# One encoder layer on one core: the last down group in token halves, and the early modulation mixed of split and unsplit chunks

## The chip, the core and the metric

The kernel runs on one core of one Trainium2 chip. The metric is the device time of one execution in microseconds; three runs of the kernel before gave 2707.13 to 2711.16 us, median 2709.91 us. All times below are microseconds from the start of the span unless marked otherwise. PE is TensorE, ACT ScalarE, DVE VectorE, POOL GpSimd and SP SyncE; here SP only issues transfers.

## The reference, cut to what matters

One layer (DEPTH = 1) over 512 prompt tokens and 32 sample tokens of width D_MODEL = 2048, in float32:

```python
mod = cs @ w_mod[li] + b_mod[li]                      # cs = silu(c), 2 rows; w_mod 2048 x 12288
sh_a, sc_a, gt_a, sh_f, sc_f, gt_f = [...]            # six pieces of 2048
h = rmsnorm(x, g_attn[li]) * (1.0 + sc_a) + sh_a
z = h @ w_in[li]
...
x = x + gt_a * o
h2 = rmsnorm(x, g_ffn[li]) * (1.0 + sc_f) + sh_f
f, cnew = conv_ffn(h2, cstate, w_up[li], conv_w[li], conv_b[li], w_down[li])
x = x + gt_f * f
y = rmsnorm(x, g_final)                               # the final norm
```

The attention between z and o and the convolution in conv_ffn are not touched. w_down is 5632 x 2048.

## The kernel before

All tokens, 544 of them, are kept transposed: 16 tiles (kt) of 128 features by 544 tokens. The large products are done as three float32r matmuls of split operands, hi x hi, hi x lo and lo x hi. For a weight chunk of 128 x 1024, ACT copies `w_raw` to `w_hi` (`hi`), and DVE subtracts that from `w_raw` to make `w_lo` (`lo`). There are four `w_raw` slots, four `w_hi` and four `w_lo`. Each engine runs its own hand-written program in order; semaphores join them.

**The early stage.** Of `w_mod` the first 32 of 96 column tiles (shift and scale of the attention norm) are done before the projection, as 64 chunks e = 0 to 63 of 512 KB, 8 to a group. PE multiplies a chunk unsplit, as float32, with `cs` (128 x 2) as the stationary operand and the chunk's two 512-column halves as moving ones. Each of these two matmuls is two records in the trace, so a chunk is four. After each group ACT copies the 2 x 512 result out (`group_out`), and PE turns it into columns (`group_columns`, L1542, after chunk 8g+1), to which DVE adds the bias (`group_mod`). While chunks 8 to 23 pass, PE also transposes x: after chunk e the tile kt = e - 8 (L1575 and L1576); ACT squares and copies it (L835, L836), DVE sums the squares. After chunk 28 PE sums them over the features (L1533), ACT takes the root (L801), DVE the reciprocal (L1205). Then DVE makes hT (`h_mul`, L1168), ACT x_hi (`h_hi`, L817) and DVE x_lo (`h_lo`, L1177) for each tile; the last four tiles wait for the last group's columns. The projection (L1584 to L1586) starts after chunk 63.

SP issues all loads in one list, `STREAM`. The load that fills a slot waits for the chunk four places earlier in the list to be used: for a modulation chunk that is `m_used`, which PE raises. Chunk e sits in slot e % 4 up to e = 61.

**The last stage.** The feed-forward part runs in 11 groups of 4 hidden tiles. The last group's down product (`down`) makes 16 output tiles n, each in two token halves (272 + 272) in turn, from 8 weight chunks. DVE adds each half into x1 (`gated`) and multiplies a finished tile by g_final (xg, L1504); ACT squares it (L1056), POOL sums the squares over the tiles (L766), PE transposes xg back to token rows (`y_turn`, L1806), and ACT copies them to `y_nat` (L1062, L1064). When all tiles are done, PE sums the squares over features for all tokens (L1821), ACT takes the root (L1083), DVE the reciprocal, and five row tiles of `y_nat` are scaled, two on ACT (L1089) and three on DVE (L1515), and stored by SP (L579, L581). The convolution's last positions (`u_rows`) are stored by POOL at the very end.

Of the kernel before, what the change touches and what calls it, by code (L numbers as in the profile page):

```python
# [223 lines left out]
W_AT = 62  # L224

# [76 lines left out]
SC0 = FC0  # L302
assert len(STREAM) % NR == FC0 % NR == EC % NR == HEAD % NR == 0
LOOP_CHUNKS = 2 * GRP * 6
LAST_DOWN = 4 * GRP + LOOP_CHUNKS * (NG - 1) // 2
ROW_COUNTS = [2 * KT, MOD_TILES, 3 * KT] + [2 * FT] * 6


def build(nc, A, O):
# [5 lines left out]
    with ctx:  # L315
# [40 lines left out]
        mod_rows = [on(st0, f"mod_rows{i}", [2, EG]) for i in range(2)]  # L356
# [37 lines left out]
        fin_st = ExitStack()  # L394
        xg = [on(fin_st, f"xg{i}", [P, T]) for i in range(2)]
        fin_st.close()
# [24 lines left out]
        f_sq, f_sum = cv, ext[1][:, 0:T]  # L421
# [24 lines left out]
        scratch_out = [sem(f"scratch_out{i}") for i in range(2)]  # L446
        ld_c, e_ev, e_t, e_tev = sem("ld_c"), sem("e_ev"), sem("e_t"), sem("e_tev")
# [45 lines left out]
        def _(sp):  # L493
            def slot_free(old):

                if old[0] == "w":
                    sp.wait_ge(s_lo, old[1] + 1)
                elif old[0] == "e":
                    sp.wait_ge(m_used, old[1] + 1)
                else:  # L500
                    sp.wait_ge(late_d, LK * (old[1] + 1))
                    sp.wait_ge(late_act, old[1] + 1)
# [74 lines left out]
            for t, ready, n in ((0, f_scd, 1), (2, f_sca, 1), (1, f_scd, 2), (3, f_sca, 2)):  # L577
                sp.wait_ge(ready, n)
                sp.dma_start(O["y_p"][0, P * t:P * t + P, :], y_nat[:, t, :]).then_inc(store, 16)  # L579
# [6 lines left out]
        def _(pool):  # L586
# [13 lines left out]
            pool.memset(minus_half, -0.5).then_inc(consts, 1)  # L600
            tiled = lambda a: a.rearrange("(k p) -> k p", p=P)
# [175 lines left out]
        def _(act):  # L777
# [18 lines left out]
            act.wait_ge(consts, 4)  # L796
# [11 lines left out]
            def hi_early(c):  # L808
                if c >= NW:
                    act.wait_ge(g_done, 2 * ((c - NW) // 2) + 2)  # L810
                hi(c, RAW_OF[("w", c)] % NR, LOADED[("w", c)])
# [9 lines left out]
            def group_out(g):  # L821

                act.wait_ge(m_used, EPG * (g + 1))
                if g >= 2:
                    act.wait_ge(e_t, g - 1)
                act.activation(mod_rows[g % 2][:, :], bank(7 - g % 2)[0:2, :], ACT.Copy).then_inc(e_ev, 1)

            for kt in range(KT):
                if (X_AT + kt) % EPG == 0:
                    group_out((X_AT + kt) // EPG - 1)  # L830
# [6 lines left out]
                if kt == 0:  # L837
# [7 lines left out]
            for kt in range(EGT, 2 * EGT):  # L845
                h_hi(kt)
            group_out(4)
            group_out(5)
            for kt in range(2 * EGT, 3 * EGT):
                h_hi(kt)  # L850
            group_out(6)
            hi_early(0)
            hi_early(1)
            group_out(7)
# [196 lines left out]
            def squares(kts):  # L1051
                for kt in kts:
                    act.wait_ge(d_ev, 4 + 8 * GRP * (NG - 1) + 2 * kt + 2)
                    if kt >= 2:
                        act.wait_ge(f_add, kt - 1)
                    act.activation(f_sq[kt % 2][:, 0:T], x1[:, kt, :], ACT.Square).then_inc(f_square, 1)  # L1056

            def y_out(kts):
                for kt in kts:
                    act.wait_ge(f_t, kt + 1)  # L1060
                    b = 2 * (kt % 2)
                    act.activation(y_nat[:, 0:QT, P * kt:P * kt + P],  # L1062
                                   bank(b)[:, :].rearrange("p (t n) -> p t n", n=P), ACT.Copy)
                    act.activation(y_nat[0:TS, QT, P * kt:P * kt + P], bank(b + 1)[0:TS, 0:P], ACT.Copy  # L1064
                                   ).then_inc(f_ev, 1)


            base = 8 * GRP * (NG - 1)
            act.wait_ge(d_done, base - 4)
            hi_ffn((LAST_DOWN + 2, None))  # L1070
            act.wait_ge(d_done, base)
            hi_ffn((LAST_DOWN + 3, None))
            for n in range(8):
                if n + 4 < 8:
                    act.wait_ge(d_done, base + 4 * (n + 1))
                    hi_ffn((LAST_DOWN + n + 4, None))
                squares(range(2 * n, 2 * n + 2))
                if n:
                    y_out(range(2 * n - 2, 2 * n))
            y_out(range(KT - 2, KT))  # L1080

            act.wait_ge(f_sum_t, 1)
            act.activation(tiny[:, 8:8 + QT], bank(0)[:, 0:QT], ACT.Sqrt, bias=eps, scale=1.0 / D)  # L1083
            act.activation(tiny[0:TS, 8 + QT:9 + QT], bank(0)[0:TS, QT:QT + 1], ACT.Sqrt, bias=eps[0:TS, :],
                           scale=1.0 / D).then_inc(f_sd, 1)
            act.wait_ge(f_rs, 1)
            act.wait_ge(f_ev, KT)
            for t in (2, 3):
                act.activation(y_nat[:, t, :], y_nat[:, t, :], ACT.Copy, scale=tiny[:, 8 + t:9 + t]).then_inc(f_sca, 1)  # L1089

            act.wait_ge(uc_t, 1)
            act.activation(u_rows[0:2 * FT, :, :].rearrange("p r n -> p (r n)"), bank(3)[0:2 * FT, :], ACT.Copy
                           ).then_inc(uc_ev, 1)
# [3 lines left out]
        def _(dve):  # L1097
# [83 lines left out]

            dve.wait_ge(rows_t, len(ROW_COUNTS))
            for i in range(1, len(ROW_COUNTS)):
                row_out(i)
            dve.wait_ge(ld_small, 80)
            for i in range(2):
                a, b = lam[2 * i], lam[2 * i + 1]
                dve.tensor_tensor_reduce(a[:, :], a[:, :], b[:, :], 1.0, 0.0, ALU.mult, ALU.add,
                                         tiny[:, 6 + i:7 + i]).then_inc(lam_dot, 1)
            dve.wait_ge(rows_ev, len(ROW_COUNTS))  # L1190
            group_mod(0)
            for kt in range(1, KT):
# [6 lines left out]
            dve.wait_ge(lam_exp, 1)  # L1199
            step(dve.tensor_tensor(tiny[:, 3:4], tiny[:, 5:6], tiny[:, 4:5], ALU.subtract))  # L1200
            step(dve.tensor_scalar(neg_lam, tiny[:, 3:4], -LAMBDA_INIT, None, ALU.add))
            group_mod(1)
            group_mod(2)
            dve.wait_ge(sd_ok, 1)
            dve.reciprocal(n0_rstd[:, :], n0_rstd[:, :]).then_inc(rs_ok, 1)  # L1205
            dve.wait_ge(rs_ok, 1)
            for q in range(4):
                for g in range(max(3, 2 * q), 2 * q + 2):
                    if g == E_GROUPS - 1:
                        lo(0, RAW_OF[("w", 0)] % NR, 0)  # L1210
                        lo(1, RAW_OF[("w", 1)] % NR, 1)
                    group_mod(g)
                dve.wait_ge(mod_ok, q + 1)
                for kt in range(EGT * q, EGT * q + EGT):
                    h_mul(kt)
                    if kt >= 2:
                        h_lo(kt - 2)
            h_lo(KT - 2)
            h_lo(KT - 1)

            def lo_early(c):
                lo(c, RAW_OF[("w", c)] % NR, c)
# [271 lines left out]

            lo_ffn((LAST_DOWN + 2, None))
            lo_ffn((LAST_DOWN + 3, None))
            for n in range(8):
                for q in range(4 * (n % 2), 4 * (n % 2) + 4):
                    down_out(q, n // 2, GRP * (NG - 1) + n // 2)
                for kt in (2 * n, 2 * n + 1):  # L1500
                    dve.wait_ge(d_ev, 4 + 8 * GRP * (NG - 1) + 2 * kt + 2)
                    if kt >= 2:
                        dve.wait_ge(f_t, kt - 1)
                    dve.tensor_scalar(xg[kt % 2][:, :], x1[:, kt, :], cols[:, GT, 2 * KT + kt:2 * KT + kt + 1], None,  # L1504
                                      ALU.mult).then_inc(f_mul, 1)
                if n + 4 < 8:
                    lo_ffn((LAST_DOWN + n + 4, None))
            dve.wait_ge(f_sd, 1)
            dve.reciprocal(tiny[:, 8:8 + QT], tiny[:, 8:8 + QT])
# [346 lines left out]
```

## Time and profile before

| what | value |
|---|---|
| median of the three runs | 2709.91 us |
| the profiled execution's own time | 2706.82 us |
| its span | 2705.0 us |
| PE busy, share of the span | 2619.0 us, 97% |
| DVE, ACT, POOL busy | 60%, 35%, 19% |
| first projection product on PE | 156.2 us |
| last product of the last down group starts | 2681.5 us |
| scaling of the output rows starts | 2688.0 us |

The profiled execution spends 1.82 us outside its span. A share of busy time is a mean over stages of different limits: this change is in the first 165 and the last 80 of 2705 us, and only what ends last there counts.

### The profile page before, as it was taken

To read this page: it belongs to the slowest core of one execution; us is meant where nothing else is said; L and a number is where in the kernel's file an instruction comes from. 1 tells how busy PE (TensorE), PEld (TensorE's weight loads), DVE (VectorE), ACT (ScalarE), POOL (GpSimd) and SP (SyncE) were. 2 spreads that over 40 slices of the span, in tenths; PEclk is the share of its full clock that TensorE was granted. 3 is DMA by queue.
4 is the path that set the end of the run, shared out by engine and by line. 5 is a ranking of instruction groups with operands and counts; after the bars stand their busy time and mean duration, and the time that the engine had idled before them with its cause. 6 is when DMAs were issued, how large, how long until landed. Compare 5 with 4: busy or idle time off the path is not lost.

```text
span 2705.0 us, 50278 instructions
## 1 busy us (share of the span) xinstructions
PE 2619.0 (97%) x19783; PEld 2448.8 (91%) x19783; DVE 1634.6 (60%) x3210; ACT 958.4 (35%) x1871; POOL 524.9 (19%) x461
## 2 busy tenths in 40 slices
PE   7999999999999999999999999999999999999997
PEld 2268889898988999899999999999999999999997
DVE  1469889874357888965554555555455555445554
ACT  2236666664344335422222222222222222222224
POOL 1057777761003452400000000000000000000003
PEclk9999999999999999999999999999999999999998
DMA  8886556562215654432332332233232223223231
GB/s 256 265 266 192 172 181 182 171 161 60 59 48 160 172 164 125 148 110 81 92 94 84 90 93 80 80 94 94 79 94 83 82 88 94 87 86 94 79 94 70
DMA packets 416210, 324.96 MB, mean 120 GB/s; under 512 B 44410, under 2 KB 360218, under 8 KB 414880
## 3 DMA queue, kind: packets, MB, share of 16 engines
q1 hardware_dynamic: 410032, 302.55, 37.6%
q0 software_dynamic: 5248, 14.56, 1.7%
q10 hardware_dynamic: 688, 4.47, 0.5%
q8 instruction: 169, 2.77, 0.4%
q14 instruction: 73, 0.60, 0.1%
HBM read 307.67 MB, written 14.07 MB: 119 GB/s over the span
## 4 chain that ended last, share of the span: by engine, by line
PE 84%; DVE 7%; DMA 3%; issue 2%; POOL 2%; ACT 1%; SPq 1%; ACTq 0%; DVEq 0%; POOLq 0%
PE ps L1584 25%; PE ps L1586 24%; PE ps L1585 24%; PE ps L1558 4%; DVE late_f L1256 3%; PE ps L1673 2%; PE ps L1639 2%; DMA w_raw<-in_w_out 2%; DMA w_raw<-in_w_mod 1%; PE ps L1657 1%; POOL oT L708 1%; DVE w_lo L1149 1%; SPq L547 1%; ACT w_hi L806 1%; PE ps L1595 1%
## 5 line engine op out<-in xcount | busy, mean ns | idle before, releaser
L1584 PE MATMUL ps<-x_hi,w_hi 128*128 128x272 f32 (+1 forms) x4480 | 1320.1, 295 | 32.1 <-DVE w_lo L1149 22.5
L1585 PE MATMUL ps<-x_lo,w_hi 128*128 128x272 f32 (+1 forms) x4480 | 1298.2, 290 | 0.0
L1586 PE MATMUL ps<-x_hi,w_lo 128*128 128x272 f32 (+1 forms) x4480 | 1296.2, 289 | 0.0
L1584 PEld LDWEIGHTS ps<-x_hi,w_hi 128*128 128x128 f32 x4480 | 850.3, 190 | 45.9 <-issue 27.6
L1586 PEld LDWEIGHTS ps<-x_hi,w_lo 128*128 128x128 f32 x4480 | 852.0, 190 | 0.0
L1585 PEld LDWEIGHTS ps<-x_lo,w_hi 128*128 128x128 f32 x4480 | 849.8, 190 | 0.0
L806 ACT ACTIVATE w_hi<-w_raw 128x1024 fp32r<-128x1024 f32 x368 | 375.0, 1052 | 1049.6 <-PE ps L1586 901.5
L1149 DVE TENSOR_TENSOR w_lo<-w_raw,w_hi 128x1024 fp32r<-128x1024 f32 x368 | 456.6, 1270 | 343.1 <-ACT w_hi L806 342.7
L1586 PE MATMUL ps<-y_hi,w_lo 128*128 128x272 f32 x1408 | 406.8, 289 | 0.0
L1584 PE MATMUL ps<-y_hi,w_hi 128*128 128x272 f32 x1408 | 406.1, 288 | 0.0
L1585 PE MATMUL ps<-y_lo,w_hi 128*128 128x272 f32 x1408 | 404.5, 287 | 0.0
L763 POOL TENSOR_TENSOR ext<-cv 128x544 f32<-128x544 f32 x1 | 1.5, 1509 | 1479.4 <-ACT cv L1056 1479.4
L1585 PEld LDWEIGHTS ps<-y_lo,w_hi 128*128 128x128 f32 x1408 | 265.3, 188 | 0.0
L1586 PEld LDWEIGHTS ps<-y_hi,w_lo 128*128 128x128 f32 x1408 | 264.7, 188 | 0.0
L1584 PEld LDWEIGHTS ps<-y_hi,w_hi 128*128 128x128 f32 x1408 | 264.6, 188 | 0.1
L1358 DVE SCALAR_TENSOR_TENSOR x<-ps,mod,x 128x272 f32<-128x272 f32 (+2 forms) x576 | 204.1, 399 | 69.8 <-PE ps L1586 69.8
L708 POOL TENSOR_TENSOR oT<-oT 128x512 f32<-128x512 f32 x150 | 223.7, 1492 | 33.7 <-ACT oT L870 25.7
L1415 DVE COPY u_shift<-ps 128x2 f32<-128x2 f32 x88 | 13.9, 158 | 307.4 <-PE ps L1586 307.4
L1256 DVE SCALAR_TENSOR_TENSOR oT<-w_raw,cs,oT 128x512 f32<-128x512 f32 x150 | 178.6, 1191 | 2.8
L708 POOL TENSOR_TENSOR late_f<-late_f 128x512 f32<-128x512 f32 x90 | 136.7, 1519 | 180.5 <-ACT late_f L870 175.8
L1558 PE MATMUL ps<-w_raw,cs 128*2 128x512 f32 x256 | 119.5, 614 | 13.8 <-DMA w_raw<-in_w_mod 13.1
L1256 DVE SCALAR_TENSOR_TENSOR late_f<-w_raw,cs,late_f 128x512 f32<-128x512 f32 x90 | 122.1, 1356 | 3.6 <-DMA w_raw<-in_w_mod 0.5
(195 smaller groups left out, 2095.8 us busy)
## 6 DMA issues: line engine op xcount, KB each, us to landing
w_raw<-in_w_mod SPq DMA_DIRECT2D x192, 512.0 KB, 4.6
w_raw<-in_w_up SPq DMA_DIRECT2D x176, 512.0 KB, 4.6
w_raw<-in_w_down SPq DMA_DIRECT2D x88, 512.0 KB, 4.2
w_raw<-in_w_in SPq DMA_DIRECT2D x56, 512.0 KB, 3.9
w_raw<-in_w_in SPq DMA_DIRECT2D x32, 256.0 KB, 3.7
w_raw<-in_w_out SPq DMA_DIRECT2D x16, 512.0 KB, 5.3
w_raw<-in_w_out SPq DMA_DIRECT2D x64, 128.0 KB, 3.9
x_transposed<-xT SPq DMA_DIRECT2D x4, 1088.0 KB, 8.6
```

The lines of the kernel that those rows point to most:

```text
L547: sp.dma_start(dst[64 * u:64 * u + 64, 4 * m:4 * m + 4, :], src.rearrange("(i p) n -> p i n", p=64)).then_inc(ld_raw[slot], 16)
L708: ins = pool.tensor_tensor(acc, late_prod(n, 0) if p == 0 and k == 1 else acc, late_prod(n, k), ALU.add)
L806: act.activation(w_hi[c % NW][:, :], w_raw[raw][:, :], ACT.Copy).then_inc(s_hi, 1)
L1149: dve.tensor_tensor(w_lo[c % NW][:, :], w_raw[raw][:, :], w_hi[c % NW][:, :].bitcast(F32), ALU.subtract).then_inc(s_lo, 1)
L1256: ins = dve.scalar_tensor_tensor(out=acc_d(g), in0=w, scalar=c, in1=acc_d(g), op0=ALU.mult, op1=ALU.add)
L1358: ins = dve.scalar_tensor_tensor(out=x1[:, n, a:a + m], in0=b[:, a - HALF[h][0]:a - HALF[h][0] + m], scalar=mod[:, gate + n, g:g + 1], in1 ...
L1558: mm = pe.matmul(bank(7 - g % 2)[0:2, :], cs[:, kt, :], w_raw[raw][:, EG * k:EG * k + EG], start=kt == 0, stop=kt == KT - 1)
L1584: pe.matmul(out[:, 0:n], hi_w, hi_x, start=first, stop=False)
L1585: pe.matmul(out[:, 0:n], hi_w, lo_x, start=False, stop=False)
L1586: return pe.matmul(out[:, 0:n], lo_w, hi_x, start=False, stop=last)
L1639: mm = pe.matmul(S[t % 2][0:np_, pc:pc + n], zq[qi % 2][r, q0:q0 + np_], kk, start=True, stop=True)
L1673: mm = pe.matmul(B7[0:np_, oc:oc + vn], probsT[0:n, tc:tc + np_], v, start=first, stop=last)
```

## The change

It has two parts.

**Early modulation.** The odd chunks from 7 to 59 (27 of 64) are split into hi and lo like the other weights, in the same `w_hi`/`w_lo` buffers, and PE multiplies them with float32r matmuls, four a chunk, against `c_parts`, 128 x 4, which holds the hi and lo parts of cs. The other chunks are still multiplied as float32, against `c_whole` (cs and two columns of zeros). The result has four rows, which `group_columns` adds by a matmul with `pair` (two stacked 2 x 2 identities) in place of a transpose. ACT and DVE get the conversions three chunks ahead (`AHEAD`), and the h work of tiles 0 to 11 is tied to places in the chunk sequence (`H_AT`). A slot of a split chunk is free when its lo part is made (`s_lo`), and not when PE has used it.

**Last down group.** All 16 tiles are done for the first 272 tokens, then all for the second (`down_last(h, n)`). The first 256 tokens' squares, root, scaling and store run beside the second half. The eight weight chunks stay on the core for both passes, the later ones in y_hi, y_lo and x_lo (`tail_w`).

```diff
+SPLIT = range(7, 60, 2)
+AHEAD = 3
+H_AT = {SUM_AT + 3: 0, SUM_AT + 4: 2, 36: 4, 37: 6, 52: 8, 53: 10}
...
                 if old[0] == "w":
-                    sp.wait_ge(s_lo, old[1] + 1)
+                    sp.wait_ge(s_lo, ES + old[1] + 1)
+                elif old[0] == "e" and old[1] in SPLIT:
+                    sp.wait_ge(s_lo, SPLIT.index(old[1]) + 1)
                 elif old[0] == "e":
                     sp.wait_ge(m_used, old[1] + 1)
...
-            group_out(2)
-            root(0, n0_rstd[:, :])
-            for kt in range(EGT):
-                h_hi(kt)
-            group_out(3)
...
+            def hi_split(e):
+
+                n = SPLIT.index(e)
+                if n >= NW:
+                    act.wait_ge(m_used, SPLIT[n - NW] + 1)
+                hi(n, RAW_OF[("e", e)] % NR, LOADED[("e", e)])
...
+            for e in range(EC):
+                if e + AHEAD in SPLIT:
+                    hi_split(e + AHEAD)
+                if e % EPG == 1 and e > EPG:
+                    group_out(e // EPG - 1)
+                if 0 <= e - X_AT < KT:
+                    x_in(e - X_AT)
...
+                if e == SUM_AT + 1:
+                    root(0, n0_rstd[:, :])
+                if e in H_AT:
+                    h_hi(H_AT[e])
+                    h_hi(H_AT[e] + 1)
...
+            for e in range(EC):
+                if e + AHEAD in SPLIT:
+                    lo_split(e + AHEAD)
...
+                if e == SUM_AT + 2:
...
+                    dve.reciprocal(n0_rstd[:, :], n0_rstd[:, :]).then_inc(rs_ok, 1)
+                    dve.wait_ge(rs_ok, 1)
+                if e in H_AT:
+                    dve.wait_ge(mod_ok, H_AT[e] // EGT + 1)
+                    h_mul(H_AT[e])
+                    h_mul(H_AT[e] + 1)
+                if e - 1 in H_AT:
+                    h_lo(H_AT[e - 1])
+                    h_lo(H_AT[e - 1] + 1)
...
+                    if e in SPLIT:
+                        n = SPLIT.index(e) % NW
+                        pe.matmul(bank(7 - g % 2)[0:4, :], c_parts[:, kt, :], w_hi[n][:, EG * k:EG * k + EG],
+                                  start=kt == 0, stop=False)
+                        mm = pe.matmul(bank(7 - g % 2)[0:4, :], c_parts[:, kt, :], w_lo[n][:, EG * k:EG * k + EG],
+                                       start=False, stop=kt == KT - 1)
+                    else:
+                        mm = pe.matmul(bank(7 - g % 2)[0:4, :], c_whole[:, kt, :], w_raw[raw][:, EG * k:EG * k + EG],
+                                       start=kt == 0, stop=kt == KT - 1)
...
+            for h in range(2):
+                for n in range(KT):
+                    down_last(h, n)
+                    if n % 2 and n > 1:
+                        y_turn(h, n - 3)
+                        y_turn(h, n - 2)
+                    if h and n == 1:
+                        y_turn(0, KT - 2)
+                        y_turn(0, KT - 1)
+                    if h and n == 3:
+                        token_sums(0)
...
+            y_turn(1, KT - 2)
+            y_turn(1, KT - 1)
+            token_sums(1)
```

What ACT has in its order from the root of the first norm on, before (in a row's brackets stand the semaphores that it waits for):

```order
L801 ACTIVATE n_rstd<-ps,tiny 128x544 [waits ss_ok]
L817 ACTIVATE x_hi<-hT,mod 128x512 [waits n_mul]
L817 ACTIVATE x_hi<-hT,mod 128x32
L817 ACTIVATE x_hi<-hT,mod 128x512 [waits n_mul]
L817 ACTIVATE x_hi<-hT,mod 128x32
L817 ACTIVATE x_hi<-hT,mod 128x512 [waits n_mul]
L817 ACTIVATE x_hi<-hT,mod 128x32
L817 ACTIVATE x_hi<-hT,mod 128x512 [waits n_mul]
L817 ACTIVATE x_hi<-hT,mod 128x32
L826 ACTIVATE mod_rows<-ps 2x512 [waits e_t,m_used]
```

The same place on ACT now; the three rows of L841 are `hi_split` of chunks 33, 35 and 37, L854 is `h_hi`, L863 `group_out(3)`:

```order
L836 ACTIVATE n_rstd<-ps,tiny 128x544 [waits ss_ok]
L841 ACTIVATE w_hi<-w_raw 128x1024 [waits ld_raw1,m_used]
L854 ACTIVATE x_hi<-hT,mod 128x512 [waits n_mul]
L854 ACTIVATE x_hi<-hT,mod 128x32
L854 ACTIVATE x_hi<-hT,mod 128x512 [waits n_mul]
L854 ACTIVATE x_hi<-hT,mod 128x32
L841 ACTIVATE w_hi<-w_raw 128x1024 [waits ld_raw3,m_used]
L854 ACTIVATE x_hi<-hT,mod 128x512 [waits n_mul]
L854 ACTIVATE x_hi<-hT,mod 128x32
L854 ACTIVATE x_hi<-hT,mod 128x512 [waits n_mul]
L854 ACTIVATE x_hi<-hT,mod 128x32
L863 ACTIVATE mod_rows<-ps 4x512 [waits e_t,m_used]
```

Conversions of weight chunks now stand between the x_hi rows, and the copy-out of group 3 stands behind a conversion and four tiles of x_hi, as before behind four tiles.

DVE from there on now (L1220 is `lo_split`: chunks 31, 33 and later 35; L1239 is `h_mul`):

```order
L1220 TENSOR_TENSOR w_lo<-w_raw,w_hi 128x1024 [waits s_hi] x2
L1289 TENSOR_TENSOR tiny<-tiny 128x1 [waits lam_exp]
L1290 TENSOR_SCALAR tiny<-tiny 128x1 [waits dve_own]
L1292 RECIPROCAL n_rstd<-n_rstd 128x544 [waits sd_ok,dve_own]
L1239 SCALAR_TENSOR_TENSOR hT<-xT,mod,n_rstd 128x512 [waits mod_ok,rs_ok]
L1239 SCALAR_TENSOR_TENSOR hT<-xT,mod,n_rstd 128x32
L1239 SCALAR_TENSOR_TENSOR hT<-xT,mod,n_rstd 128x512
L1239 SCALAR_TENSOR_TENSOR hT<-xT,mod,n_rstd 128x32
L1220 TENSOR_TENSOR w_lo<-w_raw,w_hi 128x1024 [waits s_hi]
L1239 SCALAR_TENSOR_TENSOR hT<-xT,mod,n_rstd 128x512 [waits mod_ok]
```

Before, the reciprocal stood right behind the sums of squares and two groups' columns, and nothing of the weights stood between it and hT.

The order of SP's loads from chunk 32 on now:

```order
L542 DMA w_raw<-in_w_mod 128x2x512 [waits m_used]
L542 DMA w_raw<-in_w_mod 128x2x512 [waits s_lo]
L542 DMA w_raw<-in_w_mod 128x2x512 [waits m_used]
L542 DMA w_raw<-in_w_mod 128x2x512 [waits s_lo]
```

Before, every one of them waited for `m_used` of the chunk four places earlier. Now an odd chunk's load waits for a lo part, and for the even chunk's load ahead of it in the list.

## Rows read from the trace of the kernel before

**Rows 1.** The page: busy time, share of the span, instructions, by engine.

```profile
PE 2619.0 (97%) x19783; PEld 2448.8 (91%) x19783; DVE 1634.6 (60%) x3210; ACT 958.4 (35%) x1871; POOL 524.9 (19%) x461
```

**Rows 2.** Windows: stretch and its length, busy us (instructions), granted clock, DMA share, GB/s.

```profile
36.60:76.60 40.00, 40.00 (x150) 13.30 (x150) 10.39 (x16) 19.03 (x33) 0.00 (x0) 1.00 0.70 210
97.40:140.00 42.60, 42.60 (x109) 8.76 (x108) 14.54 (x42) 9.25 (x19) 0.00 (x0) 1.00 0.86 285
```

**Rows 3.** Chain of work, start, length, what: one chunk with transposes of x.

```profile
42.93 1.81 PE ps L1558 x4
44.74 0.59 PE ps L1575 x4
45.33 0.17 PE ps L1576
```

**Rows 4.** Chain of work: one group of 8 chunks without them.

```profile
125.78 13.96 PE ps L1558 x32
```

**Rows 5.** SP's loads of w_mod, by issue in 42 to 74 us, then 99 to 148 us.

```profile
DMA to landing us min/median/max: 4.2/4.4/4.8
...
DMA to landing us min/median/max: 3.7/4.7/5.0
```

**Rows 6.** Conversions of one chunk, hi on ACT and lo on DVE, ns min/median/max.

```profile
L806 ACT ACTIVATE w_hi<-w_raw x10: 1038/1059/1064, 2602.8 to 2653.3; 128x1024 fp32r<-128x1024 f32 x10
...
L1149 DVE TENSOR_TENSOR w_lo<-w_raw,w_hi x11: 1214/1218/1225, 2599.1 to 2654.9; 128x1024 fp32r<-128x1024 f32 x11
```

**Rows 7.** Window in which PE does nothing but split products of 272 and 274 columns.

```profile
2580.00:2600.00 20.00, 20.00 (x161) 20.00 (x161) 12.22 (x24) 4.78 (x8) 0.00 (x0) 1.00 0.17 53
```

**Rows 8.** Groups by line, 0 to 190 us: x coming in on ACT.

```profile
L835 ACT ACTIVATE n_sq<-ps 128x544 f32<-128x544 f32 x16 | 10.0, 624 | 22.0 <-PE ps L1576 22.0
L836 ACT ACTIVATE xT<-ps 128x544 f32<-128x544 f32 x16 | 9.9, 618 | 0.0
```

**Rows 9.** Chain of work after chunk 28: sums, root, reciprocal, hT, columns of group 3.

```profile
85.77 1.06 PE ps L1533 x2
...
87.00 0.72 ACT n_rstd L801
...
87.75 3.56 DVE n_rstd L1205
...
91.33 2.57 DVE hT L1168 x6
...
97.05 0.40 PE ps L1542 x4
```

**Rows 10.** Chain of work around the last two chunks.

```profile
145.35 4.61 DMA w_raw<-in_w_mod
...
155.19 0.60 ACT mod_rows L826
```

**Rows 11.** Windows of the same place, with the granted clock.

```profile
143.00:149.70 6.70, 4.03 (x10) 0.68 (x8) 1.46 (x2) 2.11 (x2) 0.00 (x0) 1.00 0.95 300
149.70:153.10 3.40, 3.10 (x4) 0.47 (x5) 0.99 (x1) 0.00 (x0) 0.00 (x0) 0.51 0.77 240
```

**Rows 12.** Chain of work: the first of ACT's two scalings of 2048 elements.

```profile
2688.04 2.00 ACT y_nat L1089
```

**Rows 13.** Timeline of PE behind the last transposes.

```profile
2686.10 1.21 PE L1821 MATMUL ps<-ones,ext 128*128 128x1 f32 x10 [0.84 <-ACT y_nat L1064]
2687.23 0.68 PE L1825 MATMUL ps<-ident,u_last 128*88 128x128 f32 x4
```

**Rows 14.** Windows in the last down group, and of the stores.

```profile
2650.00:2660.00 10.00, 10.00 (x84) 9.98 (x82) 5.42 (x12) 5.82 (x13) 5.32 (x4) 1.00 0.01 2
...
2692.00:2700.00 8.00, 0.00 (x0) 0.00 (x0) 0.00 (x0) 0.42 (x1) 2.11 (x4) 0.50 1.01 392
2700.00:2703.00 3.00, 0.00 (x0) 0.00 (x0) 0.00 (x0) 0.00 (x0) 0.00 (x0) 0.50 0.83 238
2703.00:2705.00 2.00, 0.00 (x0) 0.00 (x0) 0.00 (x0) 0.00 (x0) 0.00 (x0) 0.50 0.00 0
```

More of the change, by code:

```diff
@@ L355, in build @@
         lam = [on(st0, f"lambda{i}", [P, A_DK]) for i in range(4)]
-        mod_rows = [on(st0, f"mod_rows{i}", [2, EG]) for i in range(2)]
+        mod_rows = [on(st0, f"mod_rows{i}", [4, EG]) for i in range(2)]
+        c_parts = on(st0, "c_parts", [P, KT, 4], F32R)
+        c_whole = on(st0, "c_whole", [P, KT, 4])
+        pair = on(st0, "pair", [P, 2])
         st0.close()
@@ L825, in group_out, with x_in @@
                     act.wait_ge(e_t, g - 1)
[L826 to L830, printed above, removed]
+                act.activation(mod_rows[g % 2][:, :], bank(7 - g % 2)[0:4, :], ACT.Copy).then_inc(e_ev, 1)
+            def hi_split(e):
[3 more added lines that the diff above has]
+                hi(n, RAW_OF[("e", e)] % NR, LOADED[("e", e)])
+            def x_in(kt):
                 act.wait_ge(xt_t, kt + 1)
@@ new lines, in _ @@
+            act.wait_ge(d_done, DOWN0 - 4)
+            hi_last(2)
+            act.wait_ge(d_done, DOWN0)
+            hi_last(3)
+            act.wait_ge(u_done, 4 * FT)
+            for h in range(2):
+                for n in range(8):
+                    if h == 0 and n + 4 < 8:
+                        hi_last(n + 4)
+                    for kt in (2 * n, 2 * n + 1):
+                        squares(h, kt)
+                    if n:
+                        y_out(h, 2 * n - 2)
+                        y_out(h, 2 * n - 1)
+                    elif h:
+                        y_out(0, KT - 2)
+                        y_out(0, KT - 1)
+                    if h and n == 2:
+                        final_root(0)
+                    if h and n == 4:
+                        final_scale(0)
+                    if h and n == 5:
+                        act.wait_ge(uc_t, 1)
+                        act.activation(u_rows[0:2 * FT, :, :].rearrange("p r n -> p (r n)"), bank(3)[0:2 * FT, :],
+                                       ACT.Copy).then_inc(uc_ev, 1)
@@ L1180, in h_lo, with lo_split, sum_row @@
                 ins.then_inc(x_ok, 1)
[L1182 to L1192, printed above, removed]
+            def lo_split(e):
+                n = SPLIT.index(e)
+                lo(n, RAW_OF[("e", e)] % NR, n)
+            def sum_row(kt):
                 dve.wait_ge(sq_mul, kt + 1)
@@ L1198, in _ @@
                 ins.then_inc(sq_ok if kt == KT - 1 else sq_add, 1)
[L1199 to L1217, printed above, removed]
@@ L1221, in lo_early @@
+            lo(0, RAW_OF[("w", 0)] % NR, ES)
+            lo(1, RAW_OF[("w", 1)] % NR, ES + 1)
+            group_mod(E_GROUPS - 1)
+            dve.wait_ge(mod_ok, KT // EGT)
+            for kt in range(3 * EGT, KT):
+                h_mul(kt)
+            for kt in range(3 * EGT, KT):
+                h_lo(kt)
             def lo_early(c):
-                lo(c, RAW_OF[("w", c)] % NR, c)
+                lo(c, RAW_OF[("w", c)] % NR, ES + c)
             def late_cols(tile, n, b):
@@ L1541, in group_columns @@
                 for t in range(EGT):
[L1542 to L1543 removed]
+                    mm = pe.matmul(bank(5)[:, 2 * t:2 * t + 2], mod_rows[g % 2][0:4, P * t:P * t + P], pair[0:4, :],
+                                   start=True, stop=True)
                 mm.then_inc(e_t, 1)
```

294 lines of the change are left out of this document (177 added, 117 removed).

## Prediction

> **What bounds the kernel now.** I read the page first: PE is busy 97% of the span [rows 1], so at almost any place time is gained only by taking work from PE, and lost by anything that makes PE wait. Then the windows of the early stage: with x coming in and without it PE has no idle time at full clock, at a DMA share of 0.70 and 0.86 [rows 2]. The chain of waits shows the same in single pieces: with transposes a chunk is 1.81 + 0.59 + 0.17 = 2.57 us of PE [rows 3]; without them eight are 13.96 us, 1.74 each [rows 4], 14.2 with the columns. The change takes PE work from here. So the question is what else can deliver chunks, and how fast: SP's loads [rows 5] and the conversions on ACT and DVE [rows 6].
>
> **What a split chunk saves.** In a window of nothing but split products PE starts 161 in 20.0 us [rows 7], 0.124 us for 272 columns; by columns 0.234 us for 512, so four are 0.94 us in place of 1.74. 27 chunks give 21 us back if PE never waits. The columns of a group (0.40 us) cost the same as a matmul.
>
> **How fast split chunks can come.** Let e be even. Slots e and e+1 are refilled by the loads e+4 and e+5, which stand in this order on SP; the first waits for PE to end chunk e, so the second can't go earlier either, although its slot has been free since its lo part was made. A load lands 4.4 us after its issue where the queue is light, 4.7 where it is loaded [rows 5]. At a share of 0.86 the queue moves 285 GB/s [rows 2], so full it moves 331, and the second of two loads is 524 KB / 331 GB/s = 1.6 us behind: 6.1 us after PE's end of e with the issue. Then 1.06 us hi, 1.22 us lo [rows 6] and 0.1 us of semaphores: PE can begin chunk e+5 no sooner than 8.5 us after the end of chunk e, and from there to there are four chunks. That is 4.25 us for a pair of chunks. Before, an even and an odd chunk took 5.14 us with transposes and 3.5 us without. The rule thus gives something only while x comes in (PE's own work is there 1.74 + 0.94 + 2 x 0.76 = 4.2 us a pair), and costs something in the rest. Before, the same load had three chunks of PE's time to come in, 5.2 us, with no conversion behind it.
>
> The Trainium skill (DMA: Bandwidth & Descriptors, Anatomy of one DMA) puts a DMA at about 2.0 us and bytes over 436 GB/s, 3.2 us for such a chunk. The trace has 4.4 [rows 5] and decides. By the page the rule above would give 0.1 + 3.2 + 1.2 + 2.4 = 6.9 us for two pairs, and a stretch without transposes would not grow.
>
> **The sum, by stretches of chunks, from PE's side.**
> Chunks 8 to 28: eight pairs with transposes, 8 x (4.25 - 5.14) = -7.1 us. But ACT has `group_out` behind `hi_split` of chunk 8g+3 and, at 9 and 17, behind one tile of x (0.62 + 0.62 us [rows 8]). Counted from the end of chunk 8g-2, ACT is through after 6.1 + 1.1 + 1.2 + 0.6 + 0.1 = 9.1 us, and PE, which has the columns right behind chunk 8g+1, stands there after 5.9. Three such waits (3.2, 3.2, and 2.8 without the tile of x) are +9.2. Sum +2.1.
> Chunks 29 to 33: the place in the order of ACT and DVE shown above. From the end of chunk 28: load 33 is in after 6.6 (the queue still has 31), hi and lo 33 make it 9.0; only then does DVE come to the reciprocal, 3.56 and two tiny operations: 12.9; h_mul 0 and 1 (2.57 for three, 0.86 each) 14.6; h_hi 1 15.5; hi 35 16.5; lo 35 17.8; h_mul 2 and 3 19.5; h_hi 3 20.4; `group_out` 3 21.0; columns 21.4. Before it was 97.05 + 0.40 - 85.77 = 11.7 us [rows 9], since root and reciprocal began at 87.00 and 87.75 with no conversion ahead. +9.7.
> Chunks 34 to 41: chunk 34 is 1.74, the rule brings lo 39 at 10.2; then four h_mul 3.4, h_hi 7 0.9, hi 41 1.1 (it stands behind them on ACT), lo 41 1.2: 16.9; chunk 41 and columns 18.3, against 14.2: +4.1. Chunks 50 to 57 have the same order: +4.1.
> Chunks 42 to 49: two times 8.5 is 17.0, against 14.2: +2.8.
> Chunk 58 to the last tile of the first projection product: one split chunk fewer than it costs now (-0.8); the wait for load 62 and the group's copy-out stay [rows 10], since 60 to 63 are unsplit; DVE's last four tiles no longer have h_lo 10 and 11 between them (-1.1): -1.9.
> At full clock: 2.1 + 9.7 + 4.1 + 4.1 + 2.8 - 1.9 = +20.9 us. Nothing after this stage starts by the clock on the wall: the projection, its tables and its loads all wait for x_lo, so it is passed on whole.
>
> **Clock.** Before, PE idled 3.0 us ahead of chunk 62; the granted clock was 1.00 up to there and 0.51 after, for 3.4 us in which PE was busy 3.1 [rows 11]: 1.5 us lost. The new order has some ten waits of 2 us and more. Part of such a loss falls into the next wait. Between 0 and 7 us I take 3, nearer to the row's loss twice than ten times.
>
> **Last stage.** Products, transposes and squares are as many as before; what moves to before the last product is half the norm. PE gets the first half's two sums of five, 0.5 us, and the u_rows transposes, 0.7 [rows 13]: +1.1 on its path. Behind the last product a square and four copy-outs are narrower by 256 elements each, at 1.0 ns an element of ACT [rows 12], 1.3 us, and the sums are three for five, 0.5: -1.8. Stores: the queues move 392 GB/s until 2700 and are empty from 2703 on, 2 us ahead of the end [rows 14]. Of 4.46 MB the first two tiles, 2.10 MB, are gone by then: -5.4. Sum 1.1 - 1.8 - 5.4 = -6.1. The first half's scaling on ACT (2.0 us) and DVE lies beside the second half's products, where ACT and DVE are busy 5.8 and 5.4 of 10 us [rows 14]; without that cover it costs 2 to 3. Bounds -8 and -3.
>
> Together 20.9 + 3 - 6.1 = +18 us: 2706.8 + 18 = 2724.8 by the profiled execution; that one lies 3.1 under the median, so **2728 us**.
>
> **Rivals.**
> Lighter queue: loads land in 3.7 us, the shortest of the rows, because the queue is idler at the slower pace. Each 8.5 falls to 7.8 (two pairs), the column waits by 0.7, the h chains by 0.7 each: some 6 us less, and with no clock loss +9: 2719. For it: the shortest load. Against: 4.2 is the least of 13 where the queue is light.
> Low clock in most pairs: PE is then busy under two thirds. For it: the row above. It adds up to 15 us: 2740.
> Faster: the conversions keep ahead of PE. ACT and DVE are idle for more than half of the early stage, and 27 conversions of 1.06 and 1.22 us are little. Then the x pairs give 8 x 0.95 = 7.6 us, the 18 others run into the queue at 2 x 1.6 = 3.2 us for 3.5, 5.4 us, the last stage 6.1: -19, 2691. It decides at two pairs in 7.0 us: a second load within 4.5 us of its issue, and no conversion behind an h tile. Against it are the orders shown: both chains are program order, not load.
> Only the last stage counts, if the early one comes out even: 2704.
> The page's figure for a load is the first rival's mechanism; by it the chains of h work stay, the plain stretch costs nothing: about +8, 2718.
>
> **From this to the numbers.** Forecast (up by 10 to 27 us) 0.64; lighter queue 0.14; low clock 0.09; faster, with the even case, 0.11; nothing, 0.02. Range 2708 to 2742: the loss at the short load with no clock loss and a better last stage, and the low clock; it leaves out 0.12 below and 0.06 above. The likeliest's own range is 2720 to 2737. A change under 0.2% (5.4 us) is about what a measurement here can't tell from none. Slower 0.87, same 0.02, faster 0.11.
>
> **What would show it.** First projection product some 22 us after 156.2. PE waiting for `mod_rows` at the columns of each group, 10 us or more at group 3, and for w_lo at chunks 31, 39, 41, 47, 55 and 57; pairs of 4.2 us while x comes in. Issues of odd and even loads in twos, 0.5 us apart. Scaling of the last rows 10 to 11 us before the end, not 17. The prediction fails if the second load of two lands at 4.5 us and not 6, or if DVE has the reciprocal right behind the sums.

## The result, and the profile after

The changed kernel takes 2748.68 us in the median of four runs (2746.27 to 2752.99), the kernel before beside it 2710.16: a ratio of 1.0147, interval 1.0131 to 1.0163. It is slower by 38.5 us, and the forecast was 18. The profiled execution took 2748.2 us, its span is 2746.4.

The page of the changed kernel, and its view by core:

```profile
PE 2629.1 (96%) x19815; PEld 2461.7 (90%) x19815; DVE 1668.4 (61%) x3255; ACT 989.2 (36%) x1933; POOL 529.6 (19%) x478
...
L1704 PE MATMUL ps<-x_hi,w_lo 128*128 128x272 f32 (+1 forms) x4480 | 1298.5, 290 | 7.3 <-issue 7.3
```

```profile
core 0: 2746.4 us, clock 0.980
```

PE is busy 10 us longer than in [rows 1]. Clock 0.980 is, with levels 1 and 0.5, 4% of the span at the low level, 110 us; before it was 0.990, 54 us. The 7.3 us of L1704 are new, far from both edits.

Timeline of PE in the early stage, some of the longer waits (a row's bracket: idle before, and what ended it):

```profile
38.50 3.57 PE L1676 MATMUL ps<-w_raw,c_whole 128*4 128x512 f32 x4 [4.69 <-DVE cols L1179]
...
66.43 1.05 PE L1649 MATMUL ps<-pair,mod_rows 4*128 4x2 f32 x8 [1.76 <-ACT mod_rows L863]
...
114.05 1.86 PE L1649 MATMUL ps<-pair,mod_rows 4*128 4x2 f32 x8 [10.71 <-ACT mod_rows L863]
126.88 0.39 PE L1671 MATMUL ps<-w_hi,c_parts 128*4 128x512 f32 x1 [1.92 <-DVE w_lo L1220]
133.37 0.58 PE L1671 MATMUL ps<-w_hi,c_parts 128*4 128x512 f32 x1 [3.60 <-DVE w_lo L1220]
154.37 1.05 PE L1649 MATMUL ps<-pair,mod_rows 4*128 4x2 f32 x8 [1.46 <-ACT mod_rows L863]
```

Windows of the same kernel, for chunks 34 to 41, 42 to 49 and 50 to 57 (14.2 us each before), and two stretches at low clock, around the waits of 10.71 and 3.60 us:

```profile
115.84:136.96 21.12, 15.44 (x42) 4.10 (x42) 11.72 (x25) 6.85 (x12) 0.00 (x0) 0.82 0.63 199
136.96:155.35 18.39, 15.06 (x42) 3.29 (x41) 5.04 (x6) 4.71 (x5) 0.00 (x0) 0.85 0.68 225
155.35:175.18 19.83, 14.89 (x42) 4.05 (x42) 11.79 (x24) 7.90 (x13) 0.00 (x0) 0.86 0.67 214
...
104.90:118.60 13.70, 4.55 (x12) 2.12 (x12) 10.48 (x23) 5.90 (x11) 0.00 (x0) 0.50 0.10 40
132.20:142.40 10.20, 9.03 (x21) 2.93 (x22) 5.17 (x9) 2.24 (x3) 0.00 (x0) 0.50 0.31 86
```

The first projection product starts at 193.08, before at 156.16. In the two stretches at low clock PE works at half speed: 9.03 us of work in the last row would be some 4.5 at full clock, an estimate. The wait of 1.92 us at 126.88 has no low stretch of its own. The DMA share is 0.63 to 0.68 where [rows 2] have 0.86: the queue is idler, and still each chunk is waited for.

The end of the stage for the outputs, chain of work and a window:

```profile
2733.21 0.14 PE ps L1704
...
2737.19 1.29 DVE y_nat L1602
```

```profile
2740.00:2744.00 4.00, 0.00 (x0) 0.00 (x0) 0.00 (x0) 0.00 (x0) 0.00 (x0) 0.50 1.00 412
```

From the last product to the end it is now 13.3 us, before 23.5; the scaling starts 9.2 us before the end.

Where the span's 41.4 us lie: the early stage +36.9 at the first product, +34.5 once the tiles behind it are through; +5.1 between there and the end of the first pass of the feed-forward loop, nearly all of it in 360 to 1120 us; +10.2 in the four passes after it, from one jump back to the next; -8.4 from there to the end.

### The profile page after: what moved, and what is told of

The parts are those of the page before. It is cut to its first block, busy times and chain, and to the rows that moved or that the text cites. A ratio compares the mean times of both kernels' runs of the same rounds, so it can differ in the third digit from the quotient of the medians.

```text
span 2746.4 us, 50577 instructions
## 1 busy us (share of the span) xinstructions
PE 2629.1 (96%) x19815; PEld 2461.7 (90%) x19815; DVE 1668.4 (61%) x3255; ACT 989.2 (36%) x1933; POOL 529.6 (19%) x478
## 4 chain that ended last, share of the span: by engine, by line
PE 80%; DVE 7%; DMA 5%; issue 3%; ACT 2%; POOL 2%; SPq 1%; DVEq 0%; ACTq 0%; POOLq 0%
PE ps L1702 24%; PE ps L1704 23%; PE ps L1703 23%; DVE late_f L1345 3%; DMA w_raw<-in_w_mod 2%; PE ps L1791 2%; PE ps L1757 2%; DMA w_raw<-in_w_out 2%; PE ps L1676 2%; DVE w_lo L1220 1%; ACT w_hi L841 1%; PE ps L1775 1%; POOL oT L737 1%; SPq L573 1%; DVE oT L1345 1%
## 5 line engine op out<-in xcount | busy, mean ns | idle before, releaser
L1704 PE MATMUL ps<-x_hi,w_lo 128*128 128x272 f32 (+1 forms) x4480 | 1298.5, 290 | 7.3 <-issue 7.3
L1704 PEld LDWEIGHTS ps<-x_hi,w_lo 128*128 128x128 f32 x4480 | 854.2, 191 | 0.0
L841 ACT ACTIVATE w_hi<-w_raw 128x1024 fp32r<-128x1024 f32 x389 | 397.4, 1053 | 1137.8 <-PE ps L1704 899.6
L1220 DVE TENSOR_TENSOR w_lo<-w_raw,w_hi 128x1024 fp32r<-128x1024 f32 x389 | 479.2, 1259 | 447.4 <-ACT w_hi L841 446.8
L1704 PE MATMUL ps<-y_hi,w_lo 128*128 128x272 f32 x1344 | 388.3, 289 | 0.0
L1702 PE MATMUL ps<-y_hi,w_hi 128*128 128x272 f32 x1344 | 387.7, 288 | 0.0
L1703 PE MATMUL ps<-y_lo,w_hi 128*128 128x272 f32 x1344 | 386.1, 287 | 0.0
L1703 PEld LDWEIGHTS ps<-y_lo,w_hi 128*128 128x128 f32 x1344 | 253.2, 188 | 0.0
L1704 PEld LDWEIGHTS ps<-y_hi,w_lo 128*128 128x128 f32 x1344 | 252.7, 188 | 0.0
L1702 PEld LDWEIGHTS ps<-y_hi,w_hi 128*128 128x128 f32 x1344 | 252.6, 188 | 0.0
L1447 DVE SCALAR_TENSOR_TENSOR x<-ps,mod,x 128x240 f32<-128x240 f32 (+2 forms) x576 | 204.3, 401 | 66.0 <-PE ps L1704 65.9
L1084 ACT ACTIVATE y_hi<-cv 128x512 fp32r<-128x512 f32 x88 | 33.1, 424 | 228.6 <-DVE cv L1562 228.6
```

What stands on the lines that cost most here:

```text
L841: act.activation(w_hi[c % NW][:, :], w_raw[raw][:, :], ACT.Copy).then_inc(s_hi, 1)
L1084: ins = act.activation(y_hi[par][:, jj, a:a + n], cv[1][:, a + 2 * g:a + 2 * g + n], ACT.Copy)
L1220: dve.tensor_tensor(w_lo[c % NW][:, :], w_raw[raw][:, :], w_hi[c % NW][:, :].bitcast(F32), ALU.subtract).then_inc(s_lo, 1)
L1447: ins = dve.scalar_tensor_tensor(out=x1[:, n, a:a + m], in0=b[:, a - HALF[h][0]:a - HALF[h][0] + m], scalar=mod[:, gate + n, g:g + 1], in1 ...
L1702: pe.matmul(out[:, 0:n], hi_w, hi_x, start=first, stop=False)
L1703: pe.matmul(out[:, 0:n], hi_w, lo_x, start=False, stop=False)
```

## The experiments

Each ratio is to the kernel before on the same chip. The eleven kernels made for this study ran on three chips, so across the table the ratios are the sounder numbers. What is read from a trace is one execution of each kernel. The last column tells whether PE's second idle stretch, the 7.3 us of L1704 above, is there.

| kernel | median us | ratio, interval | first product | second idle stretch in the loop |
|---|---|---|---|---|
| changed | 2748.68 | 1.0147, 1.0131 to 1.0163 | 193.1 | yes |
| tail_only | 2699.02 | 0.9966, 0.9953 to 0.9979 | 156.8 | no |
| early_only | 2751.84 | 1.0157, 1.0142 to 1.0172 | 195.9 | yes |
| split_one | 2703.82 | 0.9985, 0.9977 to 0.9994 | 160.3 | no |
| odd_first | 2717.59 | 1.0039, 1.0026 to 1.0052 | 165.5 | yes |
| tail_pad92 | 2714.19 | 1.0013, 1.0004 to 1.0021 | 159.0 | yes |
| odd_pad32 | 2712.99 | 1.0009, 0.9999 to 1.0020 | 168.1 | no |
| after_pad32 | 2737.45 | 1.0091, 1.0076 to 1.0106 | 194.9 | no |
| odd_no_h | 2715.76 | 1.0016, 1.0007 to 1.0026 | 170.4 | in two passes |
| odd_no_h_2 | 2709.87 | 0.9996, 0.9987 to 1.0004 | 162.4 | yes |
| x_splits | 2695.01 | 0.9941, 0.9929 to 0.9953 | 154.5 | no |
| x_splits_2 | 2691.74 | 0.9934, 0.9921 to 0.9946 | 149.4 | no |

**The two parts apart.** tail_only keeps the early stage of before and has the new last group; early_only is the reverse.

> Last down group of the change alone, early stage of the kernel before. The order theory (two independent parts, the early one all loss) expects the time before less what the end of the trace gave: -8.4 us, about 2702. The code-place theory (the second idle stretch of PE at the head of each loop pass comes from the 64 to 150 instructions that the early part adds to PE's program ahead of the loop) expects no such stretch here, so the feed-forward loop as before. Rival: the stretch comes from the new last stage behind the loop; then it is here too and the gain shrinks to about 0, 2710.

> Early modulation of the change alone, last group of the kernel before. If the two parts add up, 2748.7 + 8.4 = 2757. The code-place theory expects the second idle stretch of 1.7 to 1.9 us at the head of four loop passes here as in the changed kernel (7.3 us in all). If it is missing both here and with the last group alone, the cause is the sum of both and a place, not a part.

2699.0 and 2751.8, where about 2702 and 2757 were expected: the last group gives 9.3 us, the early part takes 43.5, and together that is 34 of the 38.5 measured. The parts add up within 5 us (within 7 by the ratios, which is inside their intervals).

**One split chunk in place of 27.**

```diff
-SPLIT = range(7, 60, 2)
+SPLIT = [7]
```

> Early part of the change with one split chunk (7) in place of 27; columns by the pair matmul, the new order of the h work, DVE's row copies after chunk 6, the new last group: all kept. Theory: the loss comes from the split chunks' loads and conversions in program order, so here the rule and the chains fall away: first projection product at 156.2 + 5.2 (columns 8 x 0.65) + 1 or 2 = about 163, time about 2710 with the loop's extra 7.3, 2703 without. Rival, the order of h work alone makes the wait at group 3: then the columns of group 3 still wait about 10 us and the first product is near 172.

4.8 us over tail_only, with no second stretch. The columns by fp32 matmul are 5.2 us (8 x 0.65) of work more for PE, and they are the one added cost that I see. How much of it is passed on is not settled: in the traces the first product is 3.5 us later than in tail_only, but the work at 360 us only 0.8. Timeline at group 3's columns, and groups by line for the columns in this kernel:

```profile
97.71 1.05 PE L1649 MATMUL ps<-pair,mod_rows 4*128 4x2 f32 x8 [0.65 <-ACT mod_rows L863]
```

```profile
L1649 PE MATMUL ps<-pair,mod_rows 4*128 4x2 f32 x64 | 8.4, 249 | 1.3 <-ACT mod_rows L863 1.3
```

The wait of 10.71 us is 0.65 here, so it was the conversions, not `H_AT`: the new order of the h work makes no such wait by itself. The conversions on ACT ahead of `group_out(3)` are those of chunks 33 and 35, the two rows of L841 in its order; chunk 37's stands behind it. The 64 records of eight groups are 32 in x_splits_2, where transposes make the columns:

```profile
L1656 PE MATMUL ps<-ident,mod_rows 4*128 4x4 f32 x32 | 3.2, 203 | 0.7 <-ACT mod_rows L865 0.7
```

**The odd load first.**

```diff
+for _e in range(8, 60, 2):
+    STREAM[_e], STREAM[_e + 1] = STREAM[_e + 1], STREAM[_e]
```

> The changed kernel, with the loads of each pair from (8,9) to (58,59) in the other order: the odd, split chunk first. Its load then waits behind the load that PE's end of chunk e-2 releases, two chunks earlier than now, and isn't the second of two. Theory (loads tied to PE by the list are what sets the pace): pairs without x go from 4.6 us to 3.3 to 3.6, the column waits at chunks 17 and 25 (1.8 us each) vanish, group 3's wait of 10.7 us stays within 2; first product 10 to 16 us earlier, near 180, time 2733 to 2740. Rival (the queue or the conversions themselves can't do more): pairs stay at 4.2 or more and the time within 4 us of 2749.

The largest effect of the study: two lines take 31 us off (29 by the ratios), and the first product is 27.5 us sooner, twice what I expected. Windows of this kernel, chunks 42 to 49, and its columns of group 3 in the timeline:

```profile
118.10:132.40 14.30, 12.43 (x41) 3.06 (x40) 5.00 (x7) 4.71 (x5) 0.00 (x0) 1.00 0.88 289
```

```profile
102.42 0.80 PE L1651 MATMUL ps<-pair,mod_rows 4*128 4x2 f32 x3 [9.84 <-ACT mod_rows L865]
```

Four pairs take 14.3 us, 3.6 each, where it was 18.4; the clock is 1.00, not 0.85, and the queue moves 289 GB/s, not 225. So the queue had room all along, and the loads' place in the list held it back. What I had put too low is, I think, what comes back with a wait that goes: the clock behind it. The mean clock of the span is 0.986, which is 76 us at the low level against 110, so up to 17 us of the 31, if PE is busy in all of it. Group 3's wait stays, as expected.

**No split beside the h work.**

```diff
-SPLIT = range(7, 60, 2)
+SPLIT = list(range(7, 30, 2)) + list(range(43, 52, 2))
```

> Odd loads first, and chunks 31 to 41 and 53 to 59 not split any more; splits stay for 7 to 29 and 43 to 51. The order of reciprocal, hT and x_hi on ACT and DVE has no conversion in it then. Theory (the wait at group 3's columns is the conversions of chunks 31 to 35 ahead of reciprocal and hT): that wait falls from 9.8 us to under 1.5 us and the low clock with it; first product near 153 to 156 in place of 165.5, time 2704 to 2708. Rival (H_AT puts the h work too late by itself): a wait of 5 us or more stays; split_one had 0.65 there, which speaks against it.

Half right. Group 3's wait fell from 9.84 to 1.45 us, and the time didn't follow:

```profile
98.98 1.05 PE L1651 MATMUL ps<-pair,mod_rows 4*128 4x2 f32 x8 [1.45 <-ACT mod_rows L865]
110.53 7.03 PE L1678 MATMUL ps<-w_raw,c_whole 128*4 128x512 f32 x16 [1.90 <-DMA w_raw<-in_w_mod]
119.70 1.26 PE L1651 MATMUL ps<-pair,mod_rows 4*128 4x2 f32 x8 [2.13 <-ACT mod_rows L865]
```

I had left the odd load first in pairs without a split chunk, where nothing wants it early and the even chunk's load comes late. odd_no_h_2 swaps only pairs that have a split chunk.

> odd_no_h with the odd load first only in pairs that have a split chunk. In odd_no_h group 3's wait fell from 9.8 to 1.45 us as the order theory had it, but the loss came back in the following groups (20.7 and 17.2 us for 8 chunks in place of 14.2), with waits for w_raw at even chunks. Theory: in a pair without a split the swap is itself the fault, since the even chunk's load then waits for PE's end of the odd chunk before it. So here groups 4, 6 and 7 take 14.2 to 15 us, first product 154 to 158, time 2702 to 2706. Rival (mixing split and unsplit stretches costs by itself): no change from 2715.8.

Chunks 42 to 57 take 14.2 to 14.4 us a group again, 34 to 41 take 16.1, and the first product comes 8 us earlier, at 162.4. Both miss what I expected, by 4 us each (154 to 158 and at most 2706). The early part keeps a wait of 1.65 us for DVE's row copies and one of 2.23 us at the first columns, with a low clock there. And this kernel still has the second idle stretch in the loop, which I had left out of that sum: its four passes take 1176.1 us, before 1170.9.

**The idle stretch in the loop.** Timeline of PE at the head of a pass, in the changed kernel, and under it the packets of the instruction queue in 1791 to 1793 us:

```profile
1791.46 0.39 PE L1702 MATMUL ps<-x_hi,w_hi 128*128 128x272 f32 x1 [1.34 <-issue]
1794.69 0.39 PE L1704 MATMUL ps<-x_hi,w_lo 128*128 128x272 f32 x1 [1.95 <-issue]
```

```profile
q8 instruction: 1, 0.02, 2.9%
```

Every kernel has the first idle stretch at each jump back. The second one comes 3 us later, eight matmuls into the pass, and waits for nothing that the program names. By PE's records (loads of weights, matmuls, waits, register operations) 15,922 instructions lie ahead of the loop before, 16,013 in the changed kernel: 64 more for fp32 matmuls in place of transposes, and 27 waits. tail_pad92 puts 46 small transposes (two instructions each, their result not used) ahead of PE's first product in tail_only; odd_pad32 puts 16 into odd_first, after_pad32 16 into the changed kernel (32 instructions each).

```diff
+            for _ in range(46):
+                pe.transpose(bank(3)[0:32, 0:32], ident[0:32, 0:32], ident[0:32, 0:32])
```

> The kernel with the new last group alone, and 46 transposes of 32 x 32 (a weight load and a matmul each, 92 instructions) ahead of PE's first product, where it waits for loads; their result isn't used. By the records the changed kernel has 91 more PE instructions ahead of the feed-forward loop than before (64 for fp32 matmuls in place of transposes, 27 waits), split_one 65 more. Code-place theory: the loop's body now lies where it lies in the changed kernel, so four passes show a second idle stretch of 1.4 to 1.9 us some 3 us after their start, and the time rises by 5 to 9 us, to 2704 to 2708. Rival: the second stretch comes from the early stage's timing or data; then no second stretch, 2699 plus at most 1.

> The kernel with odd loads first, and 16 such transposes ahead (32 instructions). Code-place theory: the place moves on past the one that costs the second stretch; if instructions come in blocks, 32 more put the loop's start into the next block and the second stretch goes: 5 to 9 us less than 2717.6, 2709 to 2713. Rival within the theory: the block is not passed and the stretch only moves earlier in the pass; then 2717. If the place is not the cause: 2717 to 2718 and the stretch where it was.

> The changed kernel with 16 transposes ahead of PE's first product (32 instructions), nothing else. Passes of the feed-forward loop took 294.0 to 295.4 us where the loop lies as in the changed kernel (295.4 there) and 292.6 to 293.3 elsewhere. Code-place theory: no second stretch, three passes 2.2 us shorter each, four of them 9 us, of which odd_pad32 kept 4.6 because its early part grew by 2.5: 2740 to 2745. Rival (not the place): within 2 us of 2748.7.

The head of one pass in tail_pad92, and of two passes in after_pad32:

```profile
1759.37 0.39 PE L1649 MATMUL ps<-x_hi,w_hi 128*128 128x272 f32 x1 [1.41 <-issue]
1762.18 0.29 PE L1651 MATMUL ps<-x_hi,w_lo 128*128 128x272 f32 x1 [1.54 <-issue]
```

```profile
1790.49 0.39 PE L1704 MATMUL ps<-x_hi,w_hi 128*128 128x272 f32 x1 [1.78 <-issue]
2083.30 0.39 PE L1704 MATMUL ps<-x_hi,w_hi 128*128 128x272 f32 x1 [1.72 <-issue]
```

With 16,013 instructions ahead the stretch is there, in four kernels, with a loop that has not changed by an instruction; with 32 more, 16,045, it is gone, and with 15,987 (split_one) it is not there. With 16,003 it is in two passes of four in odd_no_h and in all four in odd_no_h_2, so the place alone does not decide there. That it hangs on where the loop lies is shown. Four passes are 8.2 us shorter in after_pad32 than in the changed kernel. The whole time moved by more: by the ratios 13 us in tail_pad92, 8 in odd_pad32, 15 in after_pad32; in the first and the last that is more than I expected. Of the 16.6 us between the traces of tail_only and tail_pad92 10.9 lie in the four passes, 2 ahead of 360 us and 3.8 between 825 us and the loop's second pass. What the padding does there, in code that it only shifts, is not settled, and neither is which place costs most.

**A version that beats both.** x_splits splits chunks 9 to 23 only, with the odd load first there, DVE's row copies ahead of its first conversion, columns by transposes (DVE adds the two halves), and the new last group.

> A version meant to beat both: only chunks 9 to 23 split (while x comes in), odd loads first there, DVE's row copies ahead of its first conversion, the four-row result turned by transposes with two small additions on DVE in place of the pair matmul, new last group. Theory: eight pairs at 4.2 us in place of 5.14 are 7.6 us, less up to 1.4 for columns of groups 1 and 2 that wait; last group 9.3. First product 148.5 to 151, no second stretch in the loop, time 2691 to 2694. Rival (clock and loads give part back: 24 chunks come 7 us sooner, and the loads have to keep up with it): first product 153 or later, 2695 to 2699.

x_splits_2 moves one thing more on ACT:

```diff
-                if e + AHEAD in SPLIT:
-                    hi_split(e + AHEAD)
-                if e % EPG == 1 and e > EPG:
+                if e % EPG == 0 and e:
                     group_out(e // EPG - 1)
+                if e + AHEAD in SPLIT:
+                    hi_split(e + AHEAD)
```

> x_splits with one move on ACT: a group's copy-out stands ahead of the conversion of chunk 8g+3 and of the tile of x, not behind them. Theory (program order on ACT makes PE wait at the columns after chunks 9 and 17: 1.64 and 0.67 us, and the low clock behind the first costs 1.7 more): both waits go, first product 2.5 to 4 us earlier than 154.5, time 2691 to 2693. Rival (the copy-out was not what was late, or the conversion behind it now is): PE waits for w_lo at chunk 11 or 19 instead, time within 1 us of 2695.

2695.0 was 1 us above the range, and with a first product at 154.5 it lies where the rival had it. But the rival's cause is not there: the trace has waits of 1.64 and 0.67 us for `mod_rows` at the first two groups' columns, and none of 0.15 us or more for a load between chunk 8 and chunk 62. x_splits_2 is 0.66% faster than before, and 0.34 of that is the new last group's (tail_only). Its interval overlaps that of x_splits, so their times alone don't tell the two apart; the traces do, 149.4 against 154.5 at the first product. Windows of x_splits_2, and the only waits over 0.3 us between chunk 9 and the first product:

```profile
39.90:74.00 34.10, 34.10 (x145) 13.34 (x143) 19.53 (x30) 27.14 (x43) 0.00 (x0) 1.00 0.80 242
```

```profile
143.16 5.27 PE L1683 MATMUL ps<-w_raw,c_whole 128*4 128x512 f32 x8 [3.41 <-DMA w_raw<-in_w_mod]
149.10 0.41 PE L1656 MATMUL ps<-ident,mod_rows 4*128 4x4 f32 x4 [0.68 <-ACT mod_rows L865]
```

PE has no idle time in the first, at full clock, and the pairs are 4.2 us where they were 5.14.

## Why the prediction was right in its sign and wrong in its size

**The steps that failed.** The largest is "Nothing after this stage starts by the clock on the wall ... so it is passed on whole", which put the rest of the program at nothing: it costs 15.3 us more, 10.2 in the loop's four passes and 5.1 ahead of them. The others are two terms of the early stage that were put at nothing: the columns (5.2 us of work) and DVE's row copies ahead of chunk 8 (3.6). The clock was mis-sized too, but the loads were so in the other way.

**Right.** Both chains are program order, and the early part loses. A split chunk is 0.93 us (0.94 put). Pairs with x are 4.19 us (4.2). Group 3's wait is 10.7 us ("10 us or more"), and PE waits for w_lo at all six chunks named (0.8 to 3.6 us). From chunk 29 to the columns it is 20.5 us where 10.5 were, +10.0 for +9.7. The chain of work there reads as the forecast did, only that the conversions came 1.2 us sooner, while the columns took 1.86 us and not 0.4; that the sum comes out is in part luck. Chain of work:

```profile
94.73 4.98 DMA w_raw<-in_w_mod
...
100.88 1.23 DVE w_lo L1220
...
102.40 3.56 DVE n_rstd L1292
...
106.94 1.76 ACT x_hi L854 x4
108.70 0.95 ACT w_hi L841
...
109.68 1.23 DVE w_lo L1220
110.90 0.83 DVE hT L1239 x2
...
113.53 0.48 ACT mod_rows L863
```

**The load rule: right mechanism, wrong term.** I had the second load land 6.1 us after PE's end of chunk e, from a queue loaded as in [rows 2]. At chunk 42 it lands after 5.1, and from the end of that chunk to lo it is 7.5 us in place of 8.5:

```profile
140.56 0.37 SPq L542
...
140.97 4.63 DMA w_raw<-in_w_mod
...
145.69 1.07 ACT w_hi L841
...
146.78 1.24 DVE w_lo L1220
```

This was the rival "lighter queue", and as to loads it was right: the change itself empties the queue. That alone would have made the forecast too high. The three column waits are 4.1 us for 9.2 put. The figure of the Trainium skill that the prediction sets beside these loads (DMA: Bandwidth & Descriptors, Anatomy of one DMA) is given there for transfers that GpSimd issues; these are issued by SP, and the sum did not use it.

**Clock: right in kind, too small.** "Part of such a loss falls into the next wait. Between 0 and 7 us I take 3." Low clock covers some 56 us more of the span than before. From chunk 8 to the first product PE was busy in some 42 us of it (9.0 and 4.6 in the two rows above, the rest in stretches of 3.4 and 6.8 us), which is up to 21 us lost, less what then falls into waits. I had scaled the one loss in [rows 11], where one wait of 3 us cost 1.5. Here a wait of 1.76 us costs as much: behind the one at 66.43 a low stretch of 3.4 us follows, all of it PE's work, 1.7 us lost. No run has the clock by itself. By difference it is some 15 us, an estimate: the stage's 25.7 (below) less 20.9 put at full clock, plus some 10 that the lighter loads take off (5.1 at the columns, 1.0 to 1.2 in each of the three chains of h work, 2.0 in chunks 42 to 49).

**"The columns of a group (0.40 us) cost the same as a matmul."** False: 1.05 us, +5.2 us of PE's work in all, and 1.86 where the clock was low. I read transposes of fp32 and matmuls of fp32 as one thing. The rows had the warning: of float32, a matmul is two records and a transpose one. The Trainium skill (FP8 and Floating Point Precision, TensorE Precision Notes) says that true FP32 takes four passes through the array; the trace agrees as far as the fp32 matmul being the dearer, two records for one.

**An order that I passed over.** DVE's row copies for `cols` stand behind two conversions now, and PE waits 4.7 us for them ahead of chunk 8; +3.6 at its start. No rival had it, since I started the sum at chunk 8. With the copies ahead of the conversions, and chunk 7 not split (x_splits_2), 0.56 us is left, and that is a load.

**"Nothing after this stage starts by the clock on the wall ... passed on whole."** True for the shift, 34.3 us at 360. False for the rest of the program in two ways. The loop's four passes cost 10.2 us more; padding alone takes back 8.2 of it (after_pad32), so it is where the code lies. And 4.4 us come between 360 and 1120 us, with waits of 2.35 and 2.71 us for w_lo of w_out's chunks and a low clock behind each, in code that has not changed. It is not only kernels with a late early stage that have it: after_pad32 has 3.3 us there and early_only 1.9, but tail_pad92 and split_one, with first products at 159.0 and 160.3, have 3.0 and 1.6, and tail_only is 1.2 us shorter there than before. Why stays open.

**Last stage.** -6.1 put, -8.4 in the trace, 9.3 in the time of tail_only; the bound was -8. The stores are worth more than I took: 412 GB/s with two tiles already gone.

So the terms that I had were about right in sum: the early stage's +34.5 less 5.2 for columns and 3.6 for row copies is +25.7, where I had +23.9 with the clock. That is luck: lighter loads and a dearer clock nearly cancel. What was missing are those two, the loop (10) and the stretch before it (5). Whether columns and row copies are passed on whole is not shown.

## What to carry to other kernels

In a list that one engine issues in order, a transfer waits for everything ahead of it: ask of each slot not when it comes free but when its load can be issued, and put the transfer with the longer chain behind it first. Two lines of order were worth 31 us here, more than the 21 us that 27 split chunks could have given if PE never waited. Before moving work between engines, write down what stands behind it in each program, up to the place where the first other engine waits; and count instructions ahead of a large loop, since a change at the start can cost at the loop.

## What the runs showed of the hardware

One pass of an unchanged loop took 292.6 to 292.8 us before and 294.5 to 296.1 with 91 more instructions ahead of it, by a second idle stretch of 1.7 to 2.0 us and, in two passes of four, a low clock behind it; with 32 more it was 292.8 us in three and 294.4 in the one with a low clock. A low clock without the second stretch gives 294.3 in tail_only as well. In all thirteen traces, looked at behind the second jump back, a packet of 16,384 bytes on the instruction queue starts 1.0 us after the jump (1.6 in one), the next 4.1 to 4.7 us after it; in the changed kernel PE stands from about 5 to 7 us after the jump and goes on 1.3 to 1.5 us after the end of that packet. That fits a loop whose first block of instructions ends soon after the jump's target, so that PE runs out before the next is there; the packets are shown, the block's edge is argued. The Trainium skill (Vector Engine (DVE) Microarchitecture Reference, Instruction fetch and dispatch) gives 64 bytes an instruction, by which such a packet would be 256 instructions, an estimate; no run here was made to find the period.
